# Two-layer block on one core: order of layer 2's lifting and compression tiles, and order of twelve summing and twelve spreading matmuls of its NSA heads

## The reference, cut to what matters

```python
(nq, nkc, nvc, nks, nvs, nkw, nvw, ngate, cq, ckv, kr, bgate) = split(h @ w_in)
q_a = rope(rms_norm(heads(nq, 8)))             # NSA queries: 8 heads of 128
ks, kw = rope(rms_norm(nks)), rope(rms_norm(nkw))   # 2 + 2 heads of 128
kc = rms_norm(silu(blocks(rope(nkc)) @ cmp_k_w1) @ cmp_k_w2)   # compression, 15 blocks of 32
vc = silu(blocks(nvc) @ cmp_v_w1) @ cmp_v_w2
q_b  = (rms_norm(cq)  @ w_uq ).reshape(B, S, 8, 192)           # lifting of the MLA queries
kv_b = (rms_norm(ckv) @ w_ukv).reshape(B, S, 8, 256)           # lifting of keys and values
q_b, k_b = rms_norm(q_b), rms_norm(k_b)
o_a = nsa_mixer(q_a, kc, vc, ks, vs, kw, vw, gates);  o_b = mla_mixer(q_b, k_b, v_b)
```

## Time and profile before

| | |
|---|---|
| median of 3 runs | 1658.34 us (1657.86 to 1658.58) |
| the profiled execution: time, span | 1659.63 us, 1657.6 us |
| TensorE / VectorE / ScalarE busy | 1616.7 / 1257.2 / 823.8 us |
| granted TensorE clock, mean | 1.000 of full speed |
| layer 2's `mix` stage | 1298.9 to 1346.1 us of the span |
| NSA totals and spreads in `w_in2` | 1215.8 to 1217.7 and 1223.7 to 1226.7 us |

### The profile page before, as it was taken

One profiled execution on the slowest core, in us unless ns is written; L12 is line 12 of the kernel. 1 busy time (PEld: TensorE's weight loads), 2 busy tenths in 40 slices (PEclk: granted clock), 3 DMA queues, 4 the chain that ended last, 5 costly groups with the idle time before them and its releaser, 6 DMA issues.

```text
span 1657.6 us, 32537 instructions
## 1 busy us (share of the span) xinstructions
PE 1616.7 (98%) x11518; PEld 1427.4 (86%) x11518; DVE 1257.2 (76%) x2664; ACT 823.8 (50%) x1500; POOL 173.7 (10%) x144
## 2 busy tenths in 40 slices
PE   6999999999999999999999999999999999999998
PEld 4887988899988878888888888888889777999998
DVE  6885538859989988788888888888858165588887
ACT  3544111364469844555555555555644246544443
POOL 0020000017700000000000000000057014300000
PEclk9999999999999999999999999999999999999999
DMA  9742135855631277677767776776544651245553
GB/s 351 290 147 90 41 118 202 332 188 176 222 136 65 92 263 262 234 241 233 241 231 244 232 243 236 238 238 237 178 141 159 215 179 39 95 148 178 187 179 127
DMA packets 102624, 316.97 MB, mean 191 GB/s; under 512 B 11392, under 2 KB 21376, under 8 KB 102144
## 3 DMA queue, kind: packets, MB, share of 16 engines
q1 hardware_dynamic: 101664, 311.27, 54.2%
q10 hardware_dynamic: 864, 4.39, 0.7%
HBM read 309.71 MB, written 5.90 MB: 190 GB/s over the span
## 4 chain that ended last, share of the span: by engine, by line
PE 53%; DVE 17%; issue 15%; ACT 12%; DMA 2%; DVEq 1%; POOL 0%; ACTq 0%; SPq 0%
PE bank L501 9%; PE bank L502 9%; PE bank L503 9%; ACT whi L490 6%; DVE xn L2219 3%; PE bank L1319 3%; DVE Wlo L2202 2%; DVE arena L2208 2%; DVE wlo L495 2%; ACT arena L2049 2%; PE bank L2086 2%; PE bank L1605 2%; PE bank L2088 2%; PE bank L2090 2%; ACT arena L2040 2%
## 5 line engine op out<-in xcount | busy, mean ns | idle before, releaser
L490 ACT CAST whi<-wring 128x1024 fp32r<-128x1024 f32 x386 | 403.3, 1046 | 154.9 <-PE bank L503 85.0
L495 DVE TENSOR_TENSOR wlo<-wring,whi 128x1024 fp32r<-128x1024 f32 x341 | 415.1, 1222 | 52.5 <-ACT whi L490 43.3
L501 PE MATMUL bank<-xboth,whi 128*128 128x256 f32 x1032 | 296.0, 287 | 3.8 <-DVE wlo L495 2.2
L502 PE MATMUL bank<-xboth,whi 128*128 128x256 f32 x1032 | 291.9, 283 | 0.0
L503 PE MATMUL bank<-xboth,wlo 128*128 128x256 f32 x1032 | 291.9, 283 | 0.0
L501 PEld LDWEIGHTS bank<-xboth,whi 128*128 128x128 f32 x1032 | 197.8, 192 | 8.4 <-issue 3.8
L495 POOL TENSOR_TENSOR wlo<-wring,whi 128x1024 fp32r<-128x1024 f32 x45 | 114.9, 2560 | 812.0 <-ACT whi L490 811.9
L502 PEld LDWEIGHTS bank<-xboth,whi 128*128 128x128 f32 x1032 | 198.0, 192 | 0.6 <-issue 0.5
L503 PEld LDWEIGHTS bank<-xboth,wlo 128*128 128x128 f32 x1032 | 197.9, 192 | 0.0
L514 PE MATMUL bank<-xboth,whi 128*128 128x512 f32 x704 | 188.7, 390 | 0.0
L2086 PE MATMUL bank<-whi,Whi 128*128 128x512 f32 x512 | 159.9, 393 | 2.7 <-DVE Wlo L2202 2.7
(11 more groups left out here) (400 smaller groups left out, 2890.6 us busy)
## 6 DMA issues: line engine op xcount, KB each, us to landing
wring<-in_w SPq DMA_DIRECT2D x463, 512.0 KB, 3.6
arena<-in_ada SPq DMA_DIRECT2D x48, 512.0 KB, 6.9
xn<-in_ada SPq DMA_DIRECT2D x96, 256.0 KB, 2.7
h_spill<-arena SPq DMA_DIRECT2D x37, 128.0 KB, 2.2
arena<-h_spill SPq DMA_DIRECT2D x37, 128.0 KB, 4.2
wring<-in_w SPq DMA_DIRECT2D x6, 384.0 KB, 4.4
wring<-in_w SPq DMA_DIRECT2D x8, 256.0 KB, 3.1
arena<-in_const ACTq DMA_DIRECT2D x1, 1215.0 KB, 5.4
```

Of the source, the lines that this page charges most:

```text
L490: act.copy(whi[:, n % HSLOTS, :], wring[:, n % SLOTS, :]).then_inc(hi_ready, 1)
L495: eng.tensor_tensor(wlo[:, n % SLOTS, :], wring[:, n % SLOTS, :], whi[:, n % HSLOTS, :].bitcast(F32), ALU.subtract).then_inc(lo_ready, 1)
L501: pe.matmul(out, h, xh, start=start, stop=False, **kw)
L502: pe.matmul(out, h, xl, start=False, stop=False, **kw)
```

## The change

The list of tiles goes in twos: two lifting tiles, then two compression tiles, seven times, then `cmp_v` 6 and 7. The places of the steps between tiles stay tied to the same tiles. And the twelve matmuls of `pe_nsa_sums` and of `pe_nsa_give` are issued in other orders. No instruction is added or removed.

```diff
-MIX = [tile for pair in zip([(name, t) for name in ("uk", "uq", "uv") for t in range(COUNT[name])], BESIDE)
-       for tile in pair] + BESIDE[14:]
+LIFTED = [(name, t) for name in ("uk", "uq", "uv") for t in range(COUNT[name])]
+MIX = [tile for i in range(0, 14, 2) for tile in LIFTED[i:i + 2] + BESIDE[i:i + 2]] + BESIDE[14:]
...
         def pe_nsa_sums(pe):
...
-            for m in range(12):
+            for m in (0, 2, 4, 6, 1, 3, 5, 7, 8, 10, 9, 11):
                 g, r = (m // 2) % 4, 2 * (m // 8) + m % 2
...
         def pe_nsa_give(pe):
...
-            for m in range(12):
+            for m in (0, 2, 1, 4, 3, 6, 5, 8, 7, 9, 10, 11):
                 g, r = (m // 2) % 4, 2 * (m // 8) + m % 2
                 if m == 10:
                     pe.wait_ge(n_qn, 1)
```

## The result

The changed kernel took 1661.01 us (median of 20 runs, 1658.56 to 1663.98), the kernel before beside it 1658.64 (20 runs): a ratio of 1.0013, interval 1.0007 to 1.0019, so 1.2 to 3.2 us slower. The forecast was 1658.4, with 1656.4 to 1660.4 as its range. What came is the rival that had been given a chance of 0.05, at 1661.1: the clock falls in the longer gap. The profiled execution took 1660.53 us.

A forecast was written before the change was run, and what follows sets the result against it. The attention was taken to start at a fixed distance behind `give(2)`, with TensorE bounding the `mix` stage. Merging -1.98, `uv` 3 +1.73 and the SiLU wait +0.36 gave +0.11 us: median 1658.4 us, range 1656.4 to 1660.4.

The forecast's parts named there:

- the clock falls in the longer gap: Ahead of the attention, TensorE's 3.2 us idle time drops its clock to 1.2 GHz: 2.7 us lost, 1661.1, chance 0.05.
- The sum at `give(2)`: At the end of layer 2's `mix` stage: -1.98 + 1.73 + 0.36 = +0.11 us, delaying the attention equally.
- a pair's second `uv`: In the `mix` stage, `uv` 3 now comes ahead of `give(2)`, as the second of a pair: +1.73 us.
- The compressed keys' second layer: `compressed 0` in the `mix` stage comes sooner after the fold and waits for ScalarE's SiLU: +0.36 us, bounds 0 and 0.81.
- The six round trips: Up to `give(2)`, six fewer changes between whole-array and column-grouped work, 0.33 us each: -1.98 us.
- The first bound: For merging tiles ahead of `give(2)`: nothing is saved if each tile keeps its length; the other bound was 1.98 us.
- No load is waited for: Tile loads in the `mix` stage: counted as nothing; a wait for one there would show the forecast wrong.
- The totals and spreads: Twelve-matmul orders in `w_in2`: 0 for both; gains bounded by -0.2 and -0.38, a loss by one step of 0.22 us.
- that rule: Program order counts in `w_in2`: 1.3 us saved in the totals and as much in the spreads, 1655.8, chance 0.05.
- the third rival: The clock falls while TensorE waits 3.2 us ahead of the attention: 2.7 us lost, 1661.1, chance 0.05.
- the new wait: TensorE's wait at `compressed 0` for ScalarE's SiLU, ahead of `give(2)`: +0.36 us.
- the warming matmuls at the start: At the program's start, 24 took 5.49 us against 2.82 at the later rate; used to price a clock fall at 2.7 us.

The follow-up runs named there:

- orders alone: The kernel before with only the two new matmul orders in the totals and spreads of `w_in2`, old tile list: 1658.75 us against 1658.97, ratio 0.9996.
- no SiLU wait: Changed kernel with `give(2)` behind `uv` 2, plus `compressed 0` and sums 2 moved from behind `uv` 1 to behind `v` 2: 1656.23 us against 1658.78 before.
- early `give(2)`: The changed kernel with `give(2)` two tiles earlier, behind `uv` 2 in place of `v` 4: 1656.26 us against 1658.97 for the kernel before, ratio 0.9982.
- half-filled gap: The changed kernel with five unread warming matmuls in TensorE's gap ahead of the attention: 1660.22 us against 1658.78 for the kernel before, ratio 1.0005.

## Why the prediction was wrong

*What held.* The bound was read rightly: the attention starts at a fixed distance behind `give(2)`. The sum at `give(2)` was +0.11 and is +0.02. Of its terms, a pair's second `uv` is 1.73 as taken (3.65 - 1.92). The compressed keys' second layer starts 1332.63 - 1330.16 = 2.47 us after the fold, for 2.54 forecast, and 0.37 behind the place that `uv` 1 leaves it (1330.53 + 1.73), for 0.36. The six round trips are what is left: 0.02 - 1.73 - 0.37 = -2.08, for -1.98. The first bound, that merging saves nothing, is out.

*What also held.* No load is waited for in the stage; the first window's 1.38 us without a TensorE record are the start of the gap (1345.75 to 1347) and 0.13 us ahead of L2513. The totals and spreads are worth 0. The Trainium skill's "TensorE: Matmul & The Clock Gate", Part 3, "The mechanism", holds that matmuls start and end strictly in program order; the trace does not agree, with 1.94 us for the totals in the old order and 1.92 in the new, where that rule was reckoned at 4.1 and 2.8.

*The step that failed* is in the third rival: "After a gap of 2.94 us early in the program the granted clock read 1.00, so 2.4 GHz was kept; 3.2 us is a little beyond that", and the chance of 0.05 drawn from it. The forecast had the new gap right, 3.2 us, and called it harmless on the strength of one gap in one execution. So its sum could take the attention as only shifted ("and everything after it too"), while L762 to the end went from 306.95 to 309.74 us. The stretch of that early gap, which no edit touches, can be read in ten profiles, and it does not always come out so. TensorE's timeline and windows there, first before, then after:

```profile
23.29 3.67 PE L1106 MATMUL bank<-wring,xn 128*128 128x512 f32 x8 [2.47 <-ACT xn L603]
...
25.00:30.00 5.00, 2.06 (x6) 1.00 1.03 413
```

```profile
22.65 5.37 PE L1106 MATMUL bank<-wring,xn 128*128 128x512 f32 x8 [2.47 <-ACT xn L603]
29.84 3.70 PE L1106 MATMUL bank<-wring,xn 128*128 128x512 f32 x8 [1.82 <-ACT xn L603]
...
22.00:23.00 1.00, 0.35 (x1) 1.00 0.99 393
23.00:24.00 1.00, 1.00 (x3) 0.74 1.07 426
...
25.00:30.00 5.00, 3.18 (x6) 0.81 1.03 410
```

The same idle time of 2.47 us, the same eight records: 3.67 us in the one, 5.37 in the other. Of the ten profiles (the kernel before and nine others) eight have the long form, two the short, the profile before among them. It costs nothing there, since the next eight records wait for ScalarE anyway: they start at 29.91 and at 29.84. That is why no time before gave it away. A gap as long as 2.94 us stands in these two alone, where the clock had not fallen ahead of it, so the row that I argued from was the rarer case.

Nor does the length of a gap decide by itself. That second early gap left the clock at 1.00 where it was 2.94 us (before), 2.95 (orders alone) and 2.52 (no SiLU wait), but with the early `give(2)` the clock fell behind one of 1.90:

```profile
29.64 10.55 PE L1106 MATMUL bank<-wring,xn 128*128 128x512 f32 x20 [1.90 <-ACT xn L603]
...
30.00:31.00 1.00, 1.00 (x2) 0.50 1.03 410
```

The Trainium skill's "TensorE: Matmul & The Clock Gate", Part 1, warns that idle gaps between bursts of matmuls throttle the array anew; the three profiles with 3.22 to 3.33 us of idle time agree, with 0.50 granted behind each. The Trainium skill says there too that the chip's look at the activity does not start with the kernel, so that the moment of a change varies from run to run. The early stretch of the ten profiles agrees with that; they don't show its cause.

*The price came close, in part by luck.* 2.7 us was worked out from the warming matmuls at the start; L762 to the end is 2.79 longer. With +0.02 at `give(2)` that makes 2.8 where the median shows 2.37, within its interval. But no row of before said how long the half clock would last behind a gap: a fall was worth 1.7 us in the half-filled gap, and the same in the early stretch (5.37 - 3.67). And the window over those warming matmuls reads 1.00:

```profile
8.35:13.84 5.49, 5.49 (x25) 1.00 0.97 390
```

So that they ran at 1.2 GHz was argued from their length (5.49 us for 24, where 28 took 3.29 later), and the clock column does not bear it out.

In 18 of the 20 runs of the changed kernel the mean clock over the span was 0.998 or less, against 2 of the 66 runs of the kernel before that stood beside the experiments; so nearly all of them seem to have paid. That is a hint and no more: the profile with the early `give(2)` has a mean of 0.998 too, and paid nothing at the attention.

*Where the gain went.* The shorter list did bring TensorE to its wait earlier, by the 1.93 us that the gap grew. All of that became idle time, because `uv` 3 (1.73) and the new wait (0.37), now ahead of `give(2)`, used up what the merging saved there (2.08), and idle time here costs more than nothing. Slack next to a bound engine was counted as free.

## What to carry to other kernels

When TensorE's work is shortened in front of a wait, write down how long it will then idle and what follows the idle time; ahead of the attention three profiled gaps of 3.22 to 3.33 us cost 2.8 to 2.95 us each, and one of 1.90 still cost 1.7, while six profiles with at most 1.29 us there lost nothing. Move the operation that the other engine waits for ahead of the work that fills its answer: here that turned 2.4 us lost into 2.7 gained. And one place in one execution where the clock stayed up is no proof that it will: look for the same stretch in more than one profile before a chance is set by it.

## What the runs showed of the hardware that was not expected

The clock can fall after the gap is over. In the half-filled gap it read 1.00 until 1351 us, with TensorE at work since 1350.28, and only then 0.72 and 0.50. In the early stretch of the changed kernel it was the same: 1.00 up to 23 us, with TensorE at work since 22.65, and then 0.74 (the rows above).

The same program up to 30 us lost its clock after the 2.47 us gap in eight of ten executions. The mean clock of a run is no measure of the time lost: before's 0.999 comes with the same 1659 us as its rare 1.000.

From profile to profile the totals of `w_in2` move by 2.2 us (1214.23 to 1216.41 in the ten, with no edit ahead of them), while the distances behind them agree to 0.06 us where nothing was changed.
